# MLA rope: rotated halves as extra projection columns, and the two turns as a loop

## The reference

```python
proj = h @ w_in                                   # 1024 -> 512 (q) + 256 (kv) + 64 (k_r)
c_q, c_kv, k_r = jnp.split(proj, [512, 768], axis=-1)
q = (rms_norm(c_q, q_norm) @ w_uq)                # 8 heads of 128 (nope) + 64 (rope)
q_rope = apply_rope(q[..., 128:], cos, sin)
kv = (rms_norm(c_kv, kv_norm) @ w_ukv)            # 8 heads of 128 (k_nope) + 128 (v)
k_rope = apply_rope(k_r, cos, sin)
# causal softmax of (q_nope.k_nope + q_rope.k_rope) * scale, times v, then @ w_o

def apply_rope(t, cos, sin):
    t1, t2 = jnp.split(t, 2, axis=-1)
    return jnp.concatenate([t1 * cos - t2 * sin, t1 * sin + t2 * cos], axis=-1)
```

## Time and profile before

| | us |
|---|---|
| median of 3 runs | 2841.32 (2837.78 to 2842.31) |
| the profiled execution's own time | 2842.31 |
| its span, first to last instruction | 2840.5 |

### The profile page before, as it was taken

One profiled execution on the slowest core, in us unless ns is written; L12 is line 12 of the kernel. 1 busy time (PEld: TensorE's weight loads), 2 busy tenths in 40 slices (PEclk: granted clock), 3 DMA queues, 4 the chain that ended last, 5 costly groups with the idle time before them and its releaser, 6 DMA issues.

```text
span 2840.5 us, 32380 instructions
## 1 busy us (share of the span) xinstructions
PE 2661.6 (94%) x11916; PEld 2118.9 (75%) x11916; DVE 1179.5 (42%) x1890; ACT 738.0 (26%) x1186; POOL 1815.4 (64%) x904
## 2 busy tenths in 40 slices
PE   6999799997999879999799999999999999799999
PEld 4666688885788658888656778888778778588887
DVE  6443611126666361112637453434532331552433
ACT  3433300014445330011344431212220121331211
POOL 4445577775556457777533277777858657577784
PEclk9999899998999989999889999999999999899999
DMA  4121132322221122323211033332213212233332
GB/s 144 49 67 49 56 104 90 102 89 74 60 73 60 45 74 89 104 89 103 56 49 45 20 84 104 90 104 87 92 60 104 74 61 87 63 100 90 104 89 74
DMA packets 284656, 224.25 MB, mean 79 GB/s; under 512 B 14371, under 2 KB 277516, under 8 KB 284428
## 3 DMA queue, kind: packets, MB, share of 16 engines
q1 hardware_dynamic: 281648, 217.63, 25.0%
q10 hardware_dynamic: 2908, 5.24, 0.5%
HBM read 220.75 MB, written 2.10 MB: 78 GB/s over the span
## 4 chain that ended last, share of the span: by engine, by line
PE 84%; DVE 9%; ACT 3%; issue 2%; DVEq 1%; DMA 0%; POOL 0%; ACTq 0%; POOLq 0%
PE proj L539 25%; PE proj L540 25%; PE proj L541 25%; DVE F L499 2%; DVE a_lo L644 1%; PE aux L1900 1%; PE aux L445 1%; PE aux L1820 1%; PE aux L1825 1%; PE aux L1739 1%; ACT L470 1%; PE aux L1876 1%; PE aux L506 1%; DVE F L667 1%; PE proj L1679 1%
## 5 line engine op out<-in xcount | busy, mean ns | idle before, releaser
L1117 POOL TENSOR_TENSOR w_hi<-raw,small 128x1024 fp32r<-128x1024 f32 (+3 forms) x450 | 802.0, 1782 | 968.1 <-PE proj L541 948.5
L1120 POOL TENSOR_TENSOR w_lo<-raw,w_hi 128x1024 fp32r<-128x1024 f32 (+3 forms) x450 | 1017.1, 2260 | 35.3
L539 PE MATMUL proj<-a_hi,w_hi 128*128 128x512 f32 x2096 | 841.8, 402 | 73.3 <-DVE a_lo L644 42.9
L540 PE MATMUL proj<-a_lo,w_hi 128*128 128x512 f32 x2096 | 826.0, 394 | 0.0
L541 PE MATMUL proj<-a_hi,w_lo 128*128 128x512 f32 x2096 | 825.5, 394 | 0.0
L539 PEld LDWEIGHTS proj<-a_hi,w_hi 128*128 128x128 f32 x2096 | 400.4, 191 | 175.0 <-issue 77.9
L539 PE MATMUL proj<-g_hi,w_hi 128*128 128x512 f32 x1200 | 471.8, 393 | 18.5 <-DVE g_lo L526 9.7
L540 PE MATMUL proj<-g_lo,w_hi 128*128 128x512 f32 x1200 | 468.5, 390 | 0.0
L541 PE MATMUL proj<-g_hi,w_lo 128*128 128x512 f32 x1200 | 468.4, 390 | 0.0
L540 PEld LDWEIGHTS proj<-a_lo,w_hi 128*128 128x128 f32 x2096 | 400.2, 191 | 86.1 <-issue 3.9
L541 PEld LDWEIGHTS proj<-a_hi,w_lo 128*128 128x128 f32 x2096 | 399.6, 191 | 85.5
(11 more groups left out here) (250 smaller groups left out, 2147.7 us busy)
## 6 DMA issues: line engine op xcount, KB each, us to landing
raw<-in_mlp_w SPq DMA_DIRECT2D x64, 1024.0 KB, 5.3
raw<-in_f_w_up SPq DMA_DIRECT2D x88, 512.0 KB, 5.0
raw<-in_b_w_in SPq DMA_DIRECT2D x24, 1024.0 KB, 5.2
raw<-in_hgrn_w_in SPq DMA_DIRECT2D x32, 512.0 KB, 4.9
raw<-in_f_w_down SPq DMA_DIRECT2D x16, 1024.0 KB, 5.0
raw<-in_b_w_out SPq DMA_DIRECT2D x8, 1024.0 KB, 5.0
raw<-in_a_w_in SPq DMA_DIRECT2D x6, 1024.0 KB, 5.2
raw<-in_f_w_down SPq DMA_DIRECT2D x8, 768.0 KB, 4.3
```

What stands on the lines that cost most here:

```text
L539: pe.matmul(psum[r][:], w_hi[r][:, w], xh, start=k == 0, stop=False)
L540: pe.matmul(psum[r][:], w_hi[r][:, w], xl, start=False, stop=False)
L1117: pool.tensor_tensor(hi, src, zero.rearrange("p (a b) -> p a b", a=1).to_broadcast([P, s.kc, P]), ALU.subtract).then_inc(hi_split, 1)
L1120: pool.tensor_tensor(lo, src, hi.bitcast(F32), ALU.subtract).then_inc(lo_split, 1)
```

## The change

1. `st_mla_in` has an eighth unit: the k_r columns again, in halves of 32 columns with the halves exchanged.
2. Each q slab has a fourth unit: the rope columns of both heads, again with their halves exchanged. A pair of heads is then 8 units.
3. `rotate` reads two units: cos times the plain one, sin times the exchanged one, each in one instruction over 128 partitions, each releasing its own bank; then the sum.
4. The two stages of four heads become one stage of two turns, which every engine runs as a hardware loop, with registers in the semaphore values and addresses.

```diff
             Slab(DC, 1, lambda i: [(64 * r, 64, w_in[:, :, kr0:kr0 + 64]) for r in range(2)])])
+            Slab(DC, 2, lambda i: [(64 * r, 64, w_in[:, :, kr0:kr0 + 64]) for r in range(2)]
+                 + [(128 + 32 * r, 32, w_in[:, :, kr0 + 32 * (1 - r % 2):kr0 + 32 * (1 - r % 2) + 32]) for r in range(4)])])
...
+            p += [(384 + 64 * h + 32 * r, 32, uq[:, :, bass.ds(c0(h) + MLA_NOPE + 32 * (1 - r), 32)])
+                  for h in range(2) for r in range(2)]
...
-        st_mla = [stage(1, [
-            s for a in range(t, t + MLA_TURN, 2) for s in (
-                Slab(MLA_Q // P, 3, lambda i, a=a: uq_parts(a)),
+        st_mla = stage(MLA_HEADS // MLA_TURN, [
+            s for a in range(0, MLA_TURN, 2) for s in (
+                Slab(MLA_Q // P, 4, lambda i, a=a: uq_parts(i, a)),
...
-        V_AFTER = {5: 0, 7: 1, 12: 2, 13: 3}
+        V_AFTER = {6: 0, 8: 1, 14: 2, 15: 3}
...
-            def rotate(st, j, dst, done):
-
-                bank = arrived(dve, st, j)
-                dve.tensor_tensor(tmp[0], bank[:], rope_cos, ALU.mult)
-                for r in range(0, P, MLA_ROPE // 2):
-                    here = slice(r, r + MLA_ROPE // 2)
-                    other = r ^ (MLA_ROPE // 2)
-                    last = dve.tensor_tensor(tmp[1][here, :], bank[other:other + MLA_ROPE // 2, :], rope_sin[here, :], ALU.mult)
-                last.then_inc(*taken(st, j))
-                emptied(dve, st, j)
+            def rotate(st, j, i, dst, done):
+
+                for k, table in ((0, rope_cos), (1, rope_sin)):
+                    bank = arrived(dve, st, j + k, i)
+                    dve.tensor_tensor(tmp[k], bank[:], table, ALU.mult).then_inc(*taken(st, j + k))
+                emptied(dve, st, j + 1, i)
                 dve.tensor_tensor(dst, tmp[0], tmp[1], ALU.add).then_inc(done.sem, 1)
...
-            for t, st in enumerate(st_mla):
-                mla_heads(st, t)
+            turns(pe, st_mla.turns, mla_heads)
```

More of the change, by code:

```diff
@@ L315, in program @@
         kr0 = MLA_Q + MLA_KV
+        half = MLA_ROPE // 2
         st_mla_in = stage(1, [plain(mla_w_in[0], col=lambda i, c=c: c * 256) for c in range(3)] + [
-            Slab(DC, 1, lambda i: [(64 * r, 64, w_in[:, :, kr0:kr0 + 64]) for r in range(2)])])
+            Slab(DC, 2, lambda i: [(64 * r, 64, w_in[:, :, kr0:kr0 + 64]) for r in range(2)]
+                 + [(128 + 32 * r, 32, w_in[:, :, kr0 + 32 * (1 - r % 2):kr0 + 32 * (1 - r % 2) + 32]) for r in range(4)])])
         uq = kpn(mla_w_uq[0])
@@ L321, in program, with uq_parts @@
         MLA_TURN = 4
[L323 to L326, removed]
+        def uq_parts(i, a):
+            c0 = lambda h: i * (MLA_TURN * QH) + (a + h) * QH
+            p = [(128 * h, 128, uq[:, :, bass.ds(c0(h), 128)]) for h in range(2)]
+            p += [(256 + 64 * h, 64, uq[:, :, bass.ds(c0(h) + MLA_NOPE, 64)]) for h in range(2)]
+            p += [(384 + 64 * h + 32 * r, 32, uq[:, :, bass.ds(c0(h) + MLA_NOPE + 32 * (1 - r), 32)])
+                  for h in range(2) for r in range(2)]
             return p
         KVH = MLA_NOPE + MLA_V
-        st_mla = [stage(1, [
-            s for a in range(t, t + MLA_TURN, 2) for s in (
-                Slab(MLA_Q // P, 3, lambda i, a=a: uq_parts(a)),
-                plain(mla_w_ukv[0], kc=MLA_KV // P, width=2 * KVH, col=lambda i, a=a: a * KVH))])
-            for t in range(0, MLA_HEADS, MLA_TURN)]
-        PAIR = 7
+        st_mla = stage(MLA_HEADS // MLA_TURN, [
+            s for a in range(0, MLA_TURN, 2) for s in (
+                Slab(MLA_Q // P, 4, lambda i, a=a: uq_parts(i, a)),
+                plain(mla_w_ukv[0], kc=MLA_KV // P, width=2 * KVH, col=lambda i, a=a: i * (MLA_TURN * KVH) + a * KVH))])
         def square_out(w):
@@ L1165, in _, with mla_heads @@
                 s_c.round(act, tile(g_hi, c), c)
-            def mla_heads(st, i):
+            def mla_heads(i):
                 for a in range(2):
[L1169 to L1172, removed]
+                    for j, dst in ((0, qn[2 * a]), (1, qn[2 * a + 1]), (4, kn[2 * a]), (5, vT[0]), (6, kn[2 * a + 1]), (7, vT[1])):
+                        j += 8 * a
+                        bank = arrived(act, st_mla, j, i)
+                        act.copy(dst, bank[:]).then_inc(*taken(st_mla, j))
                         if j in V_AFTER:
@@ L1177, in mla_heads @@
                 at_mla.act(act, i, lambda hh: tile(a_hi, i * MLA_TURN + hh))
-            for t, st in enumerate(st_mla):
-                mla_heads(st, t)
+            turns(act, st_mla.turns, mla_heads)
             out_mla.act(act)
@@ L1386, in _, with mla_heads @@
             dve.wait_ge(tables_in, TABLES_IN)
-            def rotate(st, j, dst, done):
-                bank = arrived(dve, st, j)
-                dve.tensor_tensor(tmp[0], bank[:], rope_cos, ALU.mult)
-                for r in range(0, P, MLA_ROPE // 2):
-                    here = slice(r, r + MLA_ROPE // 2)
-                    other = r ^ (MLA_ROPE // 2)
-                    last = dve.tensor_tensor(tmp[1][here, :], bank[other:other + MLA_ROPE // 2, :], rope_sin[here, :], ALU.mult)
-                last.then_inc(*taken(st, j))
-                emptied(dve, st, j)
+            def rotate(st, j, i, dst, done):
[3 more added lines that the diff above has]
+                emptied(dve, st, j + 1, i)
                 dve.tensor_tensor(dst, tmp[0], tmp[1], ALU.add).then_inc(done.sem, 1)
             dve.wait_ge(*s_c.low.at(5))
-            rotate(st_mla_in, 6, k_rope, k_rope_ready)
+            rotate(st_mla_in, 6, 0, k_rope, k_rope_ready)
             dve.wait_ge(*k_rope_ready.at(0))
-            def mla_heads(st, i):
-                rotate(st, 2, q_rope[0], q_rope_ready)
+            def mla_heads(i):
+                rotate(st_mla, 2, i, q_rope[0], q_rope_ready)
                 dve.wait_ge(*q_rope_ready.at(0, i))
-                rotate(st, PAIR + 2, q_rope[1], q_rope_ready)
+                rotate(st_mla, 10, i, q_rope[1], q_rope_ready)
                 at_mla.dve(dve, i, lambda t: causal("causal", t % TB), lambda hh: tile(a_lo, i * MLA_TURN + hh),
                            lambda hh: tile(a_hi, i * MLA_TURN + hh))
-            for t, st in enumerate(st_mla):
-                mla_heads(st, t)
+            turns(dve, st_mla.turns, mla_heads)
             out_mla.dve(dve, mlp[0].pre)
@@ L1649, in _ @@
             units_together(pe, st_mla_in, range(2), DC, a_hi, a_lo, 0, pre_mla.ready)
-            for j in range(2, 7):
+            for j in range(2, 8):
                 unit(pe, st_mla_in, j, DC, a_hi, a_lo)
@@ L1655, in _, with mla_heads @@
                         n.sum(pe, c)
[L1657 to L1661, removed]
-                    else:
-                        unit(pe, st, j, MLA_KV // P, g_hi, g_lo, k0=4,
-                             ready=(lambda k: s_c.low.at(4 + k)) if j == 3 else None)
+            def mla_heads(i):
+                for j in range(st_mla.per):
+                    a, q = divmod(j, 8)
+                    if q < 4:
+                        unit(pe, st_mla, j, MLA_Q // P, g_hi, g_lo, i, ready=s_c.low.at if j == 0 else None)
+                    else:
+                        unit(pe, st_mla, j, MLA_KV // P, g_hi, g_lo, i, k0=4,
+                             ready=(lambda k: s_c.low.at(4 + k)) if j == 4 else None)
                     if j in V_AFTER:
                         hh = V_AFTER[j]
-                        emptied(pe, st, PAIR * (hh // 2) + 4 + 2 * (hh % 2))
+                        emptied(pe, st_mla, 8 * (hh // 2) + 5 + 2 * (hh % 2), i)
                         if hh >= 2:
```

## The result

| | before | after |
|---|---|---|
| median of 19 executions each, us | 2842.29 | 2860.53 |
| ratio of times after / before | | 1.0056, 95% interval 1.004 to 1.0074 |
| profiled execution, its own time | 2842.31 | 2859.74 |
| its span | 2840.5 | 2857.9 |

Two of the 19 executions of after were slow throughout (3095 and 3454 us, at a mean granted clock of 0.83 and 0.74 instead of 0.96 to 0.97): the ratio leaves them out, and the other 17 have a median of 2856.96 us.

What follows compares the result with a forecast made beforehand. PE was taken to pace the projections at 0.227 us a matmul. 5.44 + 10.88 - 2.69 + 0.44 = +14.07 us on the profiled 2842.31, less 0.99, gave a median of 2855.4 us, range 2848 to 2862.

Steps and rivals of the forecast that it cites:

- eighth unit less the hole: First projections: 24 added matmuls cost +5.44 us, while PE's wait for the k_r bank goes, -2.69 us.
- four q units: Projections of both head groups: a fourth unit in each of four q slabs, 12 matmuls each, 4 x 2.72 = +10.88 us.
- POOL: Weight splitting in the projections: POOL stays ahead of PE, 15.4 against 16.3 us a pair, so 0 added.
- loads, 128-byte rows: Slab loads in the projections: the added 128-byte rows land in time, covered by 2.6 us at least; 0 added.
- loop: Boundary between the two head groups: +0.44 us once, 0 inside the turns, at most +1.3 us over three places.
- The hole: First projections, ahead of the kv units: PE idle 2.69 us for k_r's bank, held by DVE's rotation; would go.
- signs of being wrong: MLA: PE waiting for `w_lo` or a load, full-clock attention over 39 us, or turn boundary over half a us.
- Assuming one of two hit: The two attentions: the lower TensorE clock strikes one of them, as before, costing 6.29 us where it strikes.
- Rivals 1 and 2: Attentions: neither hit by lower clock, +7.8, 2849.1 us, chance 0.18; or both hit, +20.4, 2861.7 us, chance 0.13.
- Rival 3: First turn's second pair: 128-byte rows land late and PE stands; +17.5, 2858.8 us; chance 0.05.
- rival 4: Attention steps: register waits make the loop cost more, 0.15 us x 32 = +4.8, 2860.2 us; chance 0.06.
- Rival 5: Second attention and first MLP's start: low-clock stretches vanish, 10.7 us in all, leaving +3.4, 2844.7 us; chance 0.05.

Runs made afterwards that it cites:

- e2: Kernel before with only the eighth unit added, k_r rotated from two banks; q units and written-out groups unchanged. Ratio to before 1.0025 (1.0006 to 1.0044).
- e1: Changed kernel with its loop undone on all engines, both turns written out, extra units kept. Ratio to before 1.005 (1.003 to 1.007), median 2852.0 us.
- e5: Changed kernel with the exchanged halves loaded plain, in 256-byte instead of 128-byte rows, so its rope values are wrong. Ratio to before 1.0048 (1.003 to 1.0066).
- e4: Changed kernel run again, nothing altered, for a second trace. Ratio to before 1.0061 (1.004 to 1.0082).
- e6: Kernel before with only DVE's k_r rotation moved ahead of the normed c_kv, no unit added. Ratio to before 0.9977 (0.9957 to 0.9998).
- e10: e6 timed once more: kernel before with the k_r rotation moved ahead of the normed c_kv. Ratio to before 1.0001 (0.9984 to 1.0018).
- e3: Changed kernel with the old k_r unit and one-bank rotation put back; fourth q units and loop stay. Ratio to before 1.0081 (1.0054 to 1.0107).
- e8: Changed kernel with ACT's and DVE's two turns written out, PE left looped. Single execution, 2859.71 us.
- e7: Changed kernel with the loop undone on PE alone, the other four engines still looped. Single execution, 2857.82 us.
- e9: Kernel before run again, nothing altered, for a second trace. Its first projections took 36.24 us instead of 34.79; no total time given.

## Why the prediction was right

Direction, size and the main mechanism held: added matmuls at full price, less one hole. The loop was sized at less than a third of what it cost, and the clock behind it was missing. Step by step, predicted and measured:

| step | predicted | measured at full clock |
|---|---|---|
| eighth unit less the hole | +5.44 - 2.69 = +2.75 | +2.44 (e2) |
| four q units | 4 x 2.72 = +10.88 | 7.88 - 2.44 = +5.44, and +5.42 (e1) |
| POOL | 0 | 0: the stretches are full at 0.227 us a matmul |
| loads, 128-byte rows | 0 | 0 (e5) |
| loop | +0.44, at most +1.3 | +0.90 and +0.64 = +1.54 (stands of after and e4, less 1.40) |
| sum | +14.07 | +14.84 |

**The units.** Two terms that share one clock and one rate were read from three units of before, and they came out to within 0.1 us: the four q units at 10.86, and the eighth, read from e2 against e6 and e10, where the hole is gone too, at 5.37 and 5.46. That PE paces this part, and that nothing hides a matmul there, was the whole argument.

**The hole.** It was 3.0 us worth, not 2.69. I had counted from the end of the last matmul ahead of it, 92.76 + 0.39, but matmuls overlap: the next would have started at 92.99, 2.86 us before 95.85. The first one behind the gap then took 0.31 us to the next start instead of 0.23 (PE of before, in order of time):

```profile
95.85 0.47 PE L539 MATMUL proj<-g_hi,w_hi 128*128 128x512 f32 x1 [2.71 <-issue]
96.16 0.40 PE L540 MATMUL proj<-g_lo,w_hi 128*128 128x512 f32 x1
```

The bank as its cause is shown by e6, where it is gone with the rotation moved and nothing else; e2 (gone) and e3 (back, and named by the trace) agree.

**The loop is the term that I mis-sized.** The prediction's *The loop* failed in its size, if within its range: I took the DSA loop's boundary less the written-out one as +0.44, for one place, and bounded it at +1.3 by three places. Measured are +0.90 at the boundary and +0.64 at the loop's exit, which was not in the sum at all. Rows 9 hid a part of the back edge: PE stood there for a copy of ACT, so the branch may have lain partly beside that wait. Two of the prediction's signs of being wrong came true here: a boundary of more than half a us over before, and an attention at full clock of over 39 us (39.28 first, 39.80 second). Both say the same thing: the first attention's excess over 38.38 is all in the stand behind it. It is worth 1.1 us of 14.8. The second sign was drawn too tight in any case, since a second attention without the loop takes 39.15.

**The clock behind the loop was not in the prediction.** I gave the clock to the attentions alone. In after, e3, e5 and e8 a stretch at the lower clock follows PE's looped boundary stand (2.10 to 2.30 us) and lengthens the second projections by 1.6 us (38.04 to 38.08 against 36.41 to 36.47); only e4 has none. Behind the exit stand (1.84 to 2.04 us) it came in two of the five, e3 and e4. Behind the fourteen stands of 1.40 to 1.60 us, in the seven traces where PE is written out, it never came. e7 and e8 point to PE's loop as what makes the difference, by one execution each; why the clock falls there, and whether it is the length of the stand that counts, stays open. On the mean of five traces that is about 4/5 x 1.6 + 2/5 x 1.7 = 2 us, for a total near 17, beside 16 (11.4 to 21.0) measured; the means over all fast executions of after and e4 (48) and of before beside them (46) differ by 16.6 us, with a standard error of 1.5. The 2 us are thus not to be told from the noise of the times, and the traces alone show them. The profiled pair adds up as well: 13.3 for the units, 1.5 for the loop, 1.6 for the clock behind it, 1.5 for a longer stretch at the lower clock in the second attention (46.90 - 39.80 against 44.71 - 39.15), less the 0.31 of the earlier start, is 17.6 of the 17.66 measured.

**The attentions.** Assuming one of two hit, as before, was the fair guess: the lower clock struck the first in e2 and e4, the second in before, e9, after, e6 and e8, both in e5 and e7, and neither in e1, e3 and e10. It strikes every version: 5 hits in the five traces with PE's loop, 6 in the seven without, so it adds scatter (single executions of one kernel differ by some 7 us, one standard deviation) and no difference that these traces can show. Its price was 5.6 us in before rather than the 6.29 I used, since an undisturbed second attention takes 39.15, not 38.38; over all the hits it lies between 4 and 9.5 us (both in e7, against 39.35 and 38.58 with the 0.20 of its stands).

**Rivals.** Rivals 1 and 2 are not separate outcomes but two ends of the scatter of one kernel. Rival 3 fell with e5 and with the stretch in which PE never stands. Of rival 4 the size was partly right and the place wrong: inside the turns nothing is lost (36.97 us of PE busy in an attention with loop and without), it is at the edges; its 0.15 us a step stood on no row. Rival 5 had no support: the stretches at the start of the first MLP do not go. Its sum also took the first of them at 1.8 us, where 3.59 - 9 x 0.227 is 1.55. The Trainium skill's rule on transfers under 512 bytes, weighed in the prediction ("DMA: Bandwidth & Descriptors", section Specifications), isn't tested by e5, whose rows of 128 and 256 bytes are both under it; between these two no penalty can be seen, and in the changed kernel none reaches PE.

## What to carry to other kernels

Where one engine paces a stretch and is full, an operation moved onto it costs its full rate, however much it saves an engine that nobody waits for: 15 instructions and 17 us of DVE were bought with 72 matmuls, 16.3 us of PE. If only one wait hurts, look first for an order that removes it: moving six DVE instructions ahead took the same hole away for nothing (e6). And in this kernel a hardware loop wasn't free where its engine started drained: count the back edge and the exit for every looped engine in the chain, and look at the clock behind the stand.

## What was not expected of the hardware

A back edge cost PE 0.70 us and a loop exit 0.44 us when the engine was drained; DVE's and ACT's loops together cost 0.20 us at each of the two places (e7, e8).

The clock fell behind stands of TensorE in some executions and not in others of the same length: behind 2.30 us in after and not in e4, behind 2.71 us in e9 and not in before.

In the second attention DVE's scaling of a row takes up to six times its quiet time while POOL splits weights. DVE and POOL of e1, and the same operation in the first attention of before, where POOL rests:

```profile
205.98 1.85 DVE L747 TENSOR_SCALAR acc<-acc,row_inv 128x128 f32<-128x128 f32 x1
207.76 0.55 DVE L735 CUSTOM_DVE_ANT_0 acc<-proj,causal 128x384 f32<-128x384 f32 x1
...
205.85 1.89 POOL L1120 TENSOR_TENSOR w_hi<-raw,small 128x1024 fp32r<-128x1024 f32 x1
207.82 2.35 POOL L1123 TENSOR_TENSOR w_lo<-raw,w_hi 128x1024 fp32r<-128x1024 f32 x1
```

```profile
127.76 0.29 DVE L744 TENSOR_SCALAR acc<-acc,row_inv 128x128 f32<-128x128 f32 x1
```

1.85 us against 0.29, and it ends when POOL's instruction ends (207.83 and 207.74), while the operation that reads PSUM right after it is not slowed. The Trainium skill, "SBUF — State Buffer", section SBUF: two separate sides, says that the two engines share a port pair which one of them holds for a whole instruction; this trace agrees. It is probably the 0.77 us that the second attention takes more than the first at full clock; no experiment here takes POOL's work away to show it.
